# Input columns loaded already turned, row factors applied behind the first projections, in a one-core decoder kernel

## The chip, the cores and the metric

One core of one Trainium2 chip. Times are device microseconds of one execution of the whole program. The median of 3 runs of the kernel before is 974.82 us (974.74 to 976.26). A measurement of this kernel can tell about 0.2% (1.95 us) from no change.

## The reference, cut to what matters

The program runs two decoder blocks, one after the other, over 256 rows of 1024 features (f32). Only the start of the first block bears on this change:

```python
h = jnp.concatenate([filler, meta, x], axis=1)        # 16 meta rows, 256 real rows
u = rms_norm(h, pre_mix_gain)                         # y = x * rsqrt(mean(x*x) + eps) * gain
proj = u @ w_in
qa, ka, va, qb, kb, vb, g = jnp.split(proj, SPLITS, axis=-1)
qa, ka, qb, kb = rope(...)                            # x1*cos - x2*sin, x2*cos + x1*sin
o_swa = windowed_gqa_sink_attention(qa, ka, va, attn_sink, pos, is_real)
o_diff = differential_attention(qb, kb, vb, lam, lambda_init, diff_subln_gain, is_key)
gates = jax.nn.sigmoid(g + b_gate)
merged = g_swa * (o_swa @ w_branch_swa) + g_diff * (o_diff @ w_branch_diff)
```

The norm multiplies each row by one number, the row factor, and each feature by a gain. The row factor can be taken out of the product: (r * x * gain) @ w = r * ((x * gain) @ w).

## The kernel before, in words

**Products.** Every matrix product is made of three products in a reduced float type: weights and activations are each split into a high part (ACT copies the f32 tile into the reduced type, `split` in `scalar`) and a low part (DVE subtracts, `split` in `vector`, line 1338), and TensorE adds high x high, high x low, low x high in PSUM (`feat`, lines 796 to 798; `ropek`, lines 920 to 922 for the first weights). Weights come from DRAM in units of 1 MB, in 4 raw buffers filled by SP's queue (line 2507), and are split in two halves of 128x1024 each into 2 buffers of high and low parts. A half is 24 matmuls of 256 columns (272 where the meta rows take part).

**Order.** `schedule()` writes one list of steps, and each engine walks through it and issues, in that order, what its part of each step is. The engines' queues are in order, so an instruction that waits holds everything behind it on its engine. A "split" step stands where `ahead` puts it: up to four halves ahead of the products, as soon as a buffer is free by the list. Works that lie beside the products are put in by `spread`: a head of attention has the stages s (scores on TensorE), s0/s1 (row maxima on DVE), x0/x1 (exponentials on ACT), n (probabilities on DVE), p0/p1 (transposes, copied out by ACT and by DVE), v (value product), t. The first head of windowed attention starts beside the fourth weights. Steps in `behind_split` come out behind the next splits.

**The head of the kernel.** SP loads X (256 rows), ACT's queue the meta rows, the identity matrix and the gains. ACT and DVE square and sum each row, DVE makes mean + eps, POOL raises it to the power -1/2 (line 2348), ACT and DVE scale the rows. TensorE turns them (line 782), ACT and DVE turn the PSUM banks into the high and low parts of the first activations R1 (lines 1958 and 1328) with the gain. Until then TensorE runs 13 idle matmuls (`keep`, line 787). Unit 0 (queries 0 and 1) is multiplied by `ropek`, unit 1 holds the keys (`rope` "ka0"), unit 2 the values (`v` "va"), unit 3 queries 2 and 3, unit 4 the first gates, unit 5 queries, unit 6 the second gates.

**Rotation.** After a product of queries or keys, ACT copies the four groups of 32 partitions crosswise out of PSUM (`rope` in `scalar`, four instructions), DVE multiplies PSUM by cos and the copy by sin (lines 1421, 1422), POOL adds (line 2360). `swap` makes a copy of the keys with their halves exchanged (ACT, four instructions). Values are copied by ACT, turned by TensorE and copied by DVE (`vt`, lines 1428 to 1434). A gate unit is two halves in one bank, then two tanh on ACT straight from PSUM. `claim` gives PSUM banks: banks 0 to 2 for the products, 3 to 7 for the heads; a claim waits for whatever still reads the bank.

On the profile's pages ACT's instructions all have line 1958 (a helper), so they are told apart by tiles: whi is a split, F<-F a swap, SD<-ps 128x272 a value copy, SE, SC or SD<-ps of 32 partitions a rotation copy.

Of the kernel before, what the change touches and what calls it, by code (L numbers as in the profile page):

```python
# [209 lines left out]
def schedule():  # L210
# [11 lines left out]
    def take(i, j):  # L222
        ahead(taken=1)
        while behind_split:
            step(*behind_split.pop(0))
        halves.append((i, j))
# [140 lines left out]
    def gates(u):  # L367
        return unit(("gate", u), "w_in", "feat", 4608 + 256 * u)
# [15 lines left out]
    va = behind(values("va", 1280, 0), ("swap",), ("setup",))  # L384
    units = [opening(), rope("ka0", 1024, 0), va, qa[1], ga[0], qa[2], ga[1], qa[3], ga[2], qb[0], vb[0], kb[0],
# [6 lines left out]
    n = len(units) * 2  # L392
# [89 lines left out]
def program(nc, A, out):  # L482
    with ExitStack() as ctx:
# [34 lines left out]
        mix_in, band_in = signal("in_mix", 16), signal("in_band", 16)  # L518
# [10 lines left out]
        swap_act, gate_act = signal("swap_act"), signal("gate_act")  # L529
# [70 lines left out]
        xmeta = F[:, 3072:3200].rearrange("p (b n) -> p b n", b=8)  # L600
        xs0 = [F[:, 0:1024], F[:, 1024:2048], F[:, 2048:3072]]
# [47 lines left out]
        def par_of(name):  # L649
# [3 lines left out]
            "n1": (X, xs0, R1, par_of("pre_mix"), "small"), "nm": (memt, xsm, R3b, par_of("g_mem"), "all"),  # L653
            "nx2": (X, xs2, R1, par_of("g_mix"), "all")}
        APART = ("nx2",)
        SOURCE = {"n1": ((x_in, 0), (x1_in, 0), (meta_in, 0)), "nm": ((mem_in, 0), (mem_in, 0)),
# [11 lines left out]

        def row_scale(s):

            return stat((s, "rs"), 2)

        def rows_of(s):
            src, xs = NORM[s][0:2]
            return [(src[:, 0, :], 128), (src[:, 1, :], 128)] + ([(metat, 16)] if s == "n1" else [])
# [92 lines left out]
        def tensor(e, counting):  # L768
# [86 lines left out]
            def turn(s, pairs=(0, 2, 4, 6)):  # L855
                xs, pool = NORM[s][1], NORM[s][4]
                if s == "n1":
                    p.wait_ge(id_in, 0)
# [18 lines left out]
            def turnm():  # L877
                B = claim("small", ("n1", "TX"), (norm_dve, ("n1", "xv")))
                for b in range(8):
                    p.wait_ge(norm_dve, ("n1", "sc", b // 4, 2))  # L880
                    t = tr(B[:, b * 16:(b + 1) * 16], xs0[2][0:16, b * 128:(b + 1) * 128])
                t.then_inc(norm_pe(("n1", "TX")))
# [19 lines left out]
            def rope(key, b, j, i, k):  # L902
                n = ROPE[key][1]
                B = claim("gemm", ("rope", k), (rope_act, k), (rope_dve, ("cos", k)))
                if n > NR:
                    p.wait_ge(norm_dve, ("n1", "lo", 8))
                feat(B[:, 0:n], i, j, R1, n, normed("n1"), ("rope", k))

            def ropek(part, i):

                hi, lo = unit(i)
                p.wait_ge(lo_split, (i, part))
                if part == 0:
                    for k in range(2):
                        claim("gemm", ("rope", k), (rope_act, k), (rope_dve, ("cos", k)))
                for kt in range(4 * part, 4 * part + 4):
                    p.wait_ge(norm_dve, ("n1", "lo", kt))
                    for k in range(2):
                        o, c = ps("rope", k)[:, 0:256], slice(k * 128, k * 128 + 128)
                        e.matmul(o, hi[:, kt, c], R1[0][:, kt, 0:256], start=kt == 0, stop=False)  # L920
                        e.matmul(o, hi[:, kt, c], R1[1][:, kt, 0:256], start=False, stop=False)
                        m = e.matmul(o, lo[:, kt, c], R1[0][:, kt, 0:256], start=False, stop=kt == 7)
                m.then_inc(gemm(("half", i, part), ("unit", i), ("rope", 0), ("rope", 1)))

            def v(key, u, j, i):
                B = claim("gemm", (key, u, j), (val_act, (key, u, j)))
                p.wait_ge(norm_dve, ("n1", "lo", 8))
# [16 lines left out]
            def swa(g, part):  # L944
                kv, x = g // 2, nth["swa", g]
                E = E2[x % 2]
                if part == "s":
                    p.wait_ge(rope_pool, ("qa", g))
                    p.wait_ge(rope_pool, ("ka0", 1))
                    p.wait_ge(swap_act, 1)  # L950
# [78 lines left out]
            def gate(u, j, i):  # L1029
                pair("gate", u, j, i, "gemm", R1, normed("n1"), (gate_act, u))  # L1030
# [284 lines left out]
            parts = {"turn": turn, "turnx": turnx, "rsb": rsb_, "rope": rope, "ropek": ropek, "turnm": turnm, "v": v, "vt": vt, "swa": swa, "diff": diff, "gate": gate, "bsw": bsw, "bdf": bdf,  # L1315
# [3 lines left out]
            keep(banks[7].t, 13, half[:, 0:1].to_broadcast([128, 128]), half[:, 0:1].to_broadcast([128, 256]))  # L1319
# [4 lines left out]
        def vector(e, counting):  # L1324
# [67 lines left out]
            def turnm():  # L1392
                d.wait_ge(norm_pe, ("n1", "TX"))
                d.wait_ge(mix_in, 0)
                e.tensor_tensor(xmeta, ps("n1", "TX")[:, 0:128].rearrange("p (b n) -> p b n", b=8),
                                par("pre_mix", 0, 8).unsqueeze(2).to_broadcast([128, 8, 16]), MUL).then_inc(norm_dve(("n1", "xv")))
                d.wait_ge(norm_act, ("n1", "xhi"))
# [1198 lines left out]
```

## Time and profile before

| what | value |
|---|---|
| median of 3 runs | 974.82 us |
| the profiled execution's own time | 975.47 us |
| its span | 973.7 us |
| granted TensorE clock, mean | 0.998 |
| busy TensorE / DVE / ACT / POOL | 97% / 70% / 54% / 13% |
| DMA, mean over the span | 159 GB/s |
| waits of TensorE, 12.9 to 100 us | one, of 0.76 us, for DVE (ahead of the second weights) |

The span runs from the first to the last instruction; the execution's own time lies 1.8 us above it. Matmuls are pipelined, so the start of one group of matmuls to the start of the next is what is compared here, not busy time. In a timeline row the columns are start, duration, engine, line, operation, out<-in, shapes, count, and in brackets the idle time before it with what ended it.

### The profile page before, as it was taken

How to read it: one execution, taken by the hardware profiler on the slowest of the kernel's cores; microseconds unless marked ns; L12 is line 12 of the kernel's file. 1: busy time of each engine (PE TensorE's matmuls, PEld its weight loads, DVE VectorE, ACT ScalarE, POOL GpSimd, SP SyncE). 2: the span in 40 equal slices, each digit the busy share in tenths (PEclk: the TensorE clock that was granted, in tenths of full speed). 3: DMA queues.
4: the chain of work that ended last, by engine and by line, in shares of the span. 5: the costliest groups of instructions: out<-in, count | busy, mean ns of one | idle time of the engine just before them, and what ended most of it. 6: DMA issues, size and time to landing. Idle time of an engine off the chain costs nothing.

```text
span 973.7 us, 15544 instructions
## 1 busy us (share of the span) xinstructions
PE 948.5 (97%) x6212; PEld 846.2 (87%) x6212; DVE 683.5 (70%) x1251; ACT 527.6 (54%) x1009; POOL 125.4 (13%) x145
## 2 busy tenths in 40 slices
PE   8999999999999999999999999799899999999997
PEld 8999888999999988888888898698699898888885
DVE  5888767777478676666667678786665577676765
ACT  6876666765456643444455786434444354444343
POOL 2211111211032000000001129610100000000001
PEclk9999999999999999999999999999999999999999
DMA  9544434234377556465547652201354445546541
GB/s 317 188 138 131 130 105 156 93 125 132 129 250 242 168 186 216 173 213 169 193 157 242 210 187 88 87 1 44 132 172 130 151 135 210 202 169 204 170 164 43
DMA packets 115864, 154.71 MB, mean 159 GB/s; under 512 B 2729, under 2 KB 98225, under 8 KB 115537
## 3 DMA queue, kind: packets, MB, share of 16 engines
q1 hardware_dynamic: 113376, 142.91, 44.0%
q0 software_dynamic: 1952, 10.42, 3.0%
q8 instruction: 49, 0.80, 0.3%
q10 hardware_dynamic: 464, 0.40, 0.2%
q14 instruction: 23, 0.18, 0.1%
HBM read 150.56 MB, written 3.16 MB: 158 GB/s over the span
## 4 chain that ended last, share of the span: by engine, by line
PE 85%; DVE 8%; ACT 5%; issue 2%; DMA 0%; POOL 0%; POOLq 0%; DVEq 0%; ACTq 0%
PE ps L820 14%; PE ps L796 8%; PE ps L798 8%; PE ps L797 8%; PE ps L821 7%; PE ps L1107 4%; PE ps L1080 4%; PE ps L1081 4%; PE ps L1082 4%; PE ps L839 3%; PE ps L841 3%; PE ps L840 3%; PE ps L782 3%; DVE wlo L1338 2%; PE ps L809 2%; PE ps L811 2%
## 5 line engine op out<-in xcount | busy, mean ns | idle before, releaser
L1338 DVE TENSOR_TENSOR wlo<-raw,whi 128x1024 fp32r<-128x1024 f32 (+1 forms) x268 | 326.8, 1237 | 161.7 <-ACT whi L1958 161.4
L1958 ACT ACTIVATE whi<-raw 128x1024 fp32r<-128x1024 f32 (+1 forms) x268 | 274.2, 1051 | 133.7 <-PE ps L821 53.8
L820 PE MATMUL ps<-R1b,whi 128*128 128x512 f32 x576 | 201.8, 393 | 0.0
L796 PE MATMUL ps<-R1b,whi 128*128 128x256 f32 (+1 forms) x592 | 173.3, 293 | 0.8 <-DVE wlo L1338 0.8
L798 PE MATMUL ps<-R1b,wlo 128*128 128x256 f32 (+1 forms) x592 | 168.3, 284 | 0.0
L797 PE MATMUL ps<-R1b,whi 128*128 128x256 f32 (+1 forms) x592 | 168.2, 284 | 0.0
L821 PE MATMUL ps<-R1b,wlo 128*128 128x256 f32 x576 | 161.4, 280 | 0.0
L820 PEld LDWEIGHTS ps<-R1b,whi 128*128 128x128 f32 x576 | 108.1, 188 | 24.7 <-issue 0.5
L796 PEld LDWEIGHTS ps<-R1b,whi 128*128 128x128 f32 x592 | 112.3, 190 | 10.1 <-issue 7.9
L798 PEld LDWEIGHTS ps<-R1b,wlo 128*128 128x128 f32 x592 | 112.5, 190 | 0.0
L797 PEld LDWEIGHTS ps<-R1b,whi 128*128 128x128 f32 x592 | 112.3, 190 | 0.2
L821 PEld LDWEIGHTS ps<-R1b,wlo 128*128 128x128 f32 x576 | 108.2, 188 | 0.6
L2348 POOL TENSOR_TENSOR st<-st 128x1 f32<-128x1 f32 (+5 forms) x28 | 23.1, 832 | 382.5 <-DVE st L1331 299.8
L1080 PE MATMUL ps<-whi,R3ah 128*128 128x512 f32 x176 | 69.0, 392 | 1.1 <-DVE wlo L1338 1.1
L1081 PE MATMUL ps<-wlo,R3ah 128*128 128x512 f32 x176 | 68.8, 391 | 0.0
L1082 PE MATMUL ps<-whi,R3al 128*128 128x512 f32 x176 | 68.5, 389 | 0.0
L1958 ACT ACTIVATE F<-F 128x512 f32<-128x512 f32 (+6 forms) x58 | 29.3, 507 | 57.2 <-DVE F L1591 53.7
L1958 ACT ACTIVATE R3ah<-F 128x512 fp32r<-128x512 f32 x22 | 13.9, 632 | 67.8 <-DVE F L1613 67.8
L1580 DVE TENSOR_REDUCE F<-ps 128x256 f32<-128x512 f32 x72 | 49.3, 684 | 0.0
L1958 ACT ACTIVATE SC<-ps 128x512 f32<-128x512 f32 (+3 forms) x78 | 33.1, 428 | 22.5 <-PE ps L798 10.4
L1080 PEld LDWEIGHTS ps<-whi,R3ah 128*128 128x128 f32 x176 | 33.0, 188 | 9.1 <-issue 1.9
L1958 ACT ACTIVATE SD<-ps 32x256 f32<-32x256 f32 (+4 forms) x54 | 21.3, 398 | 34.9 <-PE ps L1277 19.3
(293 smaller groups left out, 1800.2 us busy)
## 6 DMA issues: line engine op xcount, KB each, us to landing
raw<-in_w_in SPq DMA_DIRECT2D x34, 1024.0 KB, 5.1
raw<-in_w_ffn_in SPq DMA_DIRECT2D x22, 1024.0 KB, 5.1
raw<-in_w_ffn_out SPq DMA_DIRECT2D x11, 1024.0 KB, 5.3
raw<-in_w_gate SPq DMA_DIRECT2D x11, 1024.0 KB, 5.3
raw<-in_w_up SPq DMA_DIRECT2D x11, 1024.0 KB, 5.3
raw<-in_w_down SPq DMA_DIRECT2D x11, 1024.0 KB, 5.8
raw<-in_w_out SPq DMA_DIRECT2D x8, 1024.0 KB, 5.0
raw<-in_w_xkv SPq DMA_DIRECT2D x8, 1024.0 KB, 5.4
```

The source lines that it names most:

```text
L796: e.matmul(o, hi[:, kt, c], R[0][:, kt, 0:n], start=kt == 0, stop=False)
L797: e.matmul(o, hi[:, kt, c], R[1][:, kt, 0:n], start=False, stop=False)
L798: m = e.matmul(o, lo[:, kt, c], R[0][:, kt, 0:n], start=False, stop=kt == 7)
L820: e.matmul(B[:, :].rearrange("p (a n) -> p a n", a=2), hi[:, kt, c], R[2][:, :, kt, 0:256], start=kt == 0, stop=False)
L821: m = e.matmul(B[:, 0:256], lo[:, kt, c], R[0][:, kt, 0:256], start=False, stop=kt == 7)
L1080: e.matmul(B[:, :], Fh[:, k, c], hi[:, k, d], start=j == 0 and k == 0, stop=False)
L1081: e.matmul(B[:, :], Fh[:, k, c], lo[:, k, d], start=False, stop=False)
L1082: m = e.matmul(B[:, :], Fl[:, k, c], hi[:, k, d], start=False, stop=end and k == 1)
L1107: return e.matmul(o, a, b, start=True, stop=True)
L1338: e.tensor_tensor(half_of(wlo[i % HL], i, k), half_of(raw[i % RAW], i, k), f32(half_of(whi[i % HL], i, k)), SUB).then_inc(lo_split(i, (i, k)))
L1580: e.tensor_reduce(FSLOT[j % 2][0][:, at:at + 256], B[:, :].rearrange("p (a n) -> p n a", a=2), AX, ADD).then_inc(ffn_dve((kind, f, j, b)))
L1958: return e.activation(o, i, f, **kw)
```

## The change

- The host lays out a new input `x_cols`: the gains (8 columns), then X and the meta rows already turned, 128 partitions x 8 blocks x 272 rows. It is loaded in two pieces, the first weights in two halves between them. R1 is made straight from it: ACT makes column x gain in the reduced type, DVE the rest (`xsplit`). The row factor is no longer in R1.
- X, the identity, the cos/sin tables and all parameters are loaded behind the third weights, by SP; the meta rows behind the second, the band table behind the fourth. ACT's queue loads nothing at the start.
- The row factors are made beside the second weights' products (`rowstat`: two squares on ACT, one on DVE, one power on POOL for all rows). Three matmuls spread them along the columns (`rowtab`), DVE multiplies the cos and sin tables by them, and keeps the first 256 for the gates (`rowkeep`).
- Queries and keys get the row factor through the tables, values in the copies behind their transposes (products in place of copies), gates by a new DVE product 128x512 out of PSUM into GA (`scaled`), after which the two tanh run on GA in place.
- `scaled` stands at the beginning of the step behind the gate unit, tanh behind the next splits and what already stands behind them.
- The first four rotation products use the heads' banks. The first rotations (keys' and queries' first blocks) stand before and between the fourth weights' splits, the second ones behind the value product's second half; swap is in two parts. The fifth weights' first split, which stood ahead of the third weights' second half, stands with its second split behind that half and everything that follows it.
- The first weights' products run in the order high x high, high x low, low x high over four blocks, each with its own wait.
- 9 idle matmuls in place of 13.

```diff
     def opening():
+        def laid(k, key, b):
+            step("roped", key, b, k)
+            step("rotate", key, b, k)
         order.append(("w_in", "featk", 0, 256))
         for j in range(2):
             take(0, j)
             step("ropek", j, 0)
-            if j:
-                for b in range(2):
-                    step("roped", "qa", b, b)
-                    step("rotate", "qa", b, b)
-                state["rope"] = 2
             yield 1
+        order.append(("w_in", "feat", 1024, 256))
+        for j in range(2):
+            take(1, j, 4 - j)
+            step("ropep", "ka0", j, j, 1, 3 * j)
+            if j == 0:
+                step("rowstat")
+            else:
+                step("roped", "ka0", 0, 0)
+                step("roped", "qa", 0, 1)
+                step("setup")
+            yield 1
+        state["rope"] = 4
+        order.append(("w_in", "feat", 1280, 256))
+        take(2, 0, 2)
+        step("v", "va", 0, 0, 2)
+        step("rowtab")
+        step("rotate", "ka0", 0, 0)
+        ahead(2)
+        step("rotate", "qa", 0, 1)
+        step("rowkeep")
+        yield 1
+        take(2, 1, 3)
+        step("v", "va", 0, 1, 2)
+        step("swap", 0)
+        laid(2, "qa", 1)
+        laid(3, "ka0", 1)
+        step("swap", 1)
+        step("vt", "va", 0, 0)
+        yield 1
...
     def gates(u):
-        return unit(("gate", u), "w_in", "feat", 4608 + 256 * u)
+        yield from unit(("gate", u), "w_in", "feat", 4608 + 256 * u)
+        step("scaled", u)
+        behind_split.append(("tanh", u))
...
-    step("rows", "n1")
+    step("xsplit", 0, 4)
     ahead(1)
-    step("turn", "n1", (0, 2))
-    ahead(2)
-    step("turn", "n1", (4, 6))
-    step("turnm")
+    step("xsplit", 4, 8)
...
+            def rowtab():
+                B = claim("head", ("row0",), (norm_dve, "kept"))
+                p.wait_ge(id_in, 0)
+                p.wait_ge(norm_pool, "row0")
+                for i in range(2):
+                    mm(B[:, 128 * i:128 * i + 128], rs0[:, i:i + 1].to_broadcast([128, 128]), ident)
+                mm(B[:, 256:NT], rs0[0:16, 2:3].to_broadcast([16, 128]), ident[0:16, 0:16]).then_inc(norm_pe("row0"))
...
-            keep(banks[7].t, 13, half[:, 0:1].to_broadcast([128, 128]), half[:, 0:1].to_broadcast([128, 256]))
+            keep(banks[7].t, 9, half[:, 0:1].to_broadcast([128, 128]), half[:, 0:1].to_broadcast([128, 256]))
...
+            def xsplit(first, end):
+                for kt in range(first, end):
+                    d.wait_ge(norm_act, ("n1", "hi", kt))
+                    stt(R1[1][:, kt, :], xT[:, kt, :], xcols[:, kt:kt + 1], f32(R1[0][:, kt, :]), MUL, SUB).then_inc(
+                        norm_dve(("n1", "lo", kt)))
...
+            def scaled(u):
+                d.wait_ge(gemm, ("gate", u))
+                d.wait_ge(norm_dve, "kept")
+                e.tensor_tensor(GA[:, 2 * u:2 * u + 2, :], ps("gate", u)[:, :].rearrange("p (b n) -> p b n", b=2), rep(rsb0, 2),
+                                MUL).then_inc(gate_dve(u))
...
+            def xsplit(first, end):
+                a.wait_ge(xb_in if first else xa_in, 0)
+                for kt in range(first, end):
+                    act(R1[0][:, kt, :], xT[:, kt, :], scale=xcols[:, kt:kt + 1]).then_inc(norm_act(("n1", "hi", kt)))
...
+            def tanh(u):
+                a.wait_ge(gate_dve, u)
+                a.wait_ge(set_dve, "hb")
+                for k in range(2):
+                    act(GA[:, 2 * u + k, :], GA[:, 2 * u + k, :], ACT.Tanh, bias=hb[:, 2 * u + k:2 * u + k + 1],
+                        scale=0.5).then_inc(gate_act(u))
...
-            e.dma_start(X[:, 0, :], x_src[:, 0, :]).then_inc(x_in(0), 16)
-            e.dma_start(X[:, 1, :], x_src[:, 1, :]).then_inc(x1_in(0), 16)
+            cut = 8 + 4 * NT
+            e.dma_start(xcols[:, 0:cut], A["x_cols"][:, 0:cut]).then_inc(xa_in(0), 16)
             for i in range(len(order)):
                 src, k, n = unit_src(i)
+                dst = raw[i % RAW][:, 0:k * n].rearrange("p (k n) -> p k n", k=k)
+                if i == 0:
+                    e.dma_start(dst[:, 0:4, :], src[:, 0:4, :]).then_inc(first_in(0), 16)
+                    e.dma_start(xcols[:, cut:], A["x_cols"][:, cut:]).then_inc(xb_in(0), 16)
+                    e.dma_start(dst[:, 4:8, :], src[:, 4:8, :]).then_inc(raw_in[0](0), 16)
+                    continue
```

## Rows read from the trace of the kernel before

**Rows 1.** The page's first part: busy time, share of the span, instructions.
```profile
PE 948.5 (97%) x6212; PEld 846.2 (87%) x6212; DVE 683.5 (70%) x1251; ACT 527.6 (54%) x1009; POOL 125.4 (13%) x145
```

**Rows 2.** The chain of waits, 0 to 20 us: start us, us, what.
```profile
0.73 4.26 DMA X<-in_x
...
18.03 1.24 DVE wlo L1338
```

**Rows 3.** Timeline of SP's queue, 0 to 10 us: the first two weight loads' issue.
```profile
1.62 0.43 SPq L2507 DMA_DIRECT2D raw<-in_w_in  x1
...
3.07 0.45 SPq L2507 DMA_DIRECT2D raw<-in_w_in  x1
```

**Rows 4.** DMA view, the same two issues: KB, us from issue to landing.
```profile
raw<-in_w_in SPq DMA_DIRECT2D x1, 1024.0 KB, 8.0
...
raw<-in_w_in SPq DMA_DIRECT2D x1, 1024.0 KB, 10.2
```

**Rows 5.** Timeline of PE, 0 to 79 us: idle matmuls, products, scores, value products.
```profile
0.93 8.52 PE L787 MATMUL ps<-st 128*128 128x256 f32 x26 [0.93 <-DVE st L1946]
...
12.78 0.35 PE L920 MATMUL ps<-R1b,whi 128*128 128x256 f32 x1 [0.85 <-DVE R1b L1328]
...
19.40 0.36 PE L796 MATMUL ps<-R1b,whi 128*128 128x272 f32 x1 [0.76 <-DVE wlo L1338]
...
31.59 0.49 PE L782 MATMUL ps<-ca,SD 128*128 128x128 f32 x3
31.83 0.36 PE L796 MATMUL ps<-R1b,whi 128*128 128x256 f32 x1
...
36.68 0.39 PE L796 MATMUL ps<-R1b,whi 128*128 128x256 f32 x1
...
53.27 0.61 PE L971 MATMUL ps<-SC,SD 128*128 128x128 f32 x4
...
78.22 0.61 PE L971 MATMUL ps<-SC,SD 128*128 128x128 f32 x4
```

**Rows 6.** Timeline of ACT, 26 to 53 us.
```profile
26.95 1.63 ACT L1958 ACTIVATE SE<-ps 32x272 f32<-32x272 f32 x4
...
30.29 1.79 ACT L1958 ACTIVATE F<-F 64x272 f32<-64x272 f32 x4 [0.20 <-POOL F L2360]
...
33.44 1.05 ACT L1958 ACTIVATE whi<-raw 128x1024 fp32r<-128x1024 f32 x1
...
45.78 0.84 ACT L1958 ACTIVATE SE<-ps,st 128x256 f32<-128x256 f32 x2
...
52.34 0.60 ACT L1958 ACTIVATE SC<-ps 128x512 f32<-128x512 f32 x1
```

**Rows 7.** Timeline of DVE, 37 to 79 us.
```profile
37.15 0.42 DVE L1428 COPY F<-ps 128x256 f32<-128x256 f32 x1
...
52.04 0.69 DVE L1468 COPY SC<-ps 128x512 f32<-128x512 f32 x1
52.64 0.28 DVE L1470 COPY SC<-ps 128x128 f32<-128x128 f32 x1
52.84 0.42 DVE L1421 TENSOR_TENSOR SE<-ps,ca 128x256 f32<-128x256 f32 x1
...
77.48 0.28 DVE L1470 COPY SC<-ps 128x128 f32<-128x128 f32 x1
```

**Rows 8.** Timeline of POOL, 29 to 31 us: the sum that swap 1 waits for.
```profile
29.48 0.78 POOL L2360 TENSOR_TENSOR F<-SE 128x272 f32<-128x272 f32 x1 [1.97 <-DVE SE L1422]
```

**Rows 9.** Timeline of PE, 581 to 584 us, and the windows view of one microsecond.
```profile
581.24 1.95 PE L1107 MATMUL ps<-st,F 128*128 128x1 f32 x16
...
583.36 0.41 PE L797 MATMUL ps<-R1b,whi 128*128 128x256 f32 x1
583.58 0.41 PE L798 MATMUL ps<-R1b,wlo 128*128 128x256 f32 x1
...
583.00:584.00 1.00, 1.00 (x6) 1.00 (x6) 0.79 (x3) 0.07 (x1) 0.92 (x1) 0.55 0.07 25
```

More of the change, by code:

```diff
@@ L220, in ahead, with take @@
         step("ahead", len(halves) + n, len(halves) + taken)
-    def take(i, j):
-        ahead(taken=1)
+    def take(i, j, n=2 * HL):
+        ahead(n, 1)
         while behind_split:
@@ L517, in program @@
         x_in, x1_in, meta_in, id_in, pc_in, ca_in = [signal("in_" + n, 16) for n in ("x", "x1", "meta", "id", "pc", "ca")]
-        mix_in, band_in = signal("in_mix", 16), signal("in_band", 16)
+        xa_in, xb_in, first_in, band_in = [signal("in_" + n, 16) for n in ("xa", "xb", "first", "band")]
         cb_in, mem_in, g1_in, g2_in, g3_in = [signal("in_" + n, 16) for n in ("cb", "mem", "g1", "g2", "g3")]
@@ L903, in rope @@
                 n = ROPE[key][1]
-                B = claim("gemm", ("rope", k), (rope_act, k), (rope_dve, ("cos", k)))
-                if n > NR:
-                    p.wait_ge(norm_dve, ("n1", "lo", 8))
+                B = claim("head" if k < 4 else "gemm", ("rope", k), (rope_act, k), (rope_dve, ("cos", k)))
                 feat(B[:, 0:n], i, j, R1, n, normed("n1"), ("rope", k))
@@ L911, in ropek @@
                 hi, lo = unit(i)
-                p.wait_ge(lo_split, (i, part))
                 if part == 0:
                     for k in range(2):
[L915 to L923, printed above, removed]
+                        claim("head", ("rope", 1 + k), (rope_act, 1 + k), (rope_dve, ("cos", 1 + k)))
+                p.wait_ge(hi_split, (i, part))
+                for w, r in ((hi, 0), (hi, 1), (lo, 0)):
+                    if w is lo:
+                        p.wait_ge(lo_split, (i, part))
+                    for kt in range(4 * part, 4 * part + 4):
+                        if r:
+                            p.wait_ge(norm_dve, ("n1", "lo", kt))
+                        elif w is hi:
+                            p.wait_ge(norm_act, ("n1", "hi", kt))
+                        for k in range(2):
+                            m = e.matmul(ps("rope", 1 + k)[:, 0:256], w[:, kt, 128 * k:128 * k + 128], R1[r][:, kt, 0:256],
+                                         start=kt == 0 and r == 0 and w is hi, stop=kt == 7 and w is lo)
+                m.then_inc(gemm(("half", i, part), ("unit", i), ("rope", 1), ("rope", 2)))
             def v(key, u, j, i):
                 B = claim("gemm", (key, u, j), (val_act, (key, u, j)))
-                p.wait_ge(norm_dve, ("n1", "lo", 8))
                 feat(B[:, 0:NT], i, j, R1, NT, normed("n1"), (key, u, j))
@@ L2584 @@
     given = {n: src[n] for n in _BIG}
-    given.update(params=params, const_a=const_a, const_b=const_b)
+    columns = np.concatenate([src[n].reshape(-1, 8, 128).transpose(2, 1, 0) for n in ("x", "meta_tokens")], 2)
+    x_cols = np.concatenate([cols("pre_mix_gain"), columns.reshape(128, 8 * NT)], 1)
+    given.update(params=params, const_a=const_a, const_b=const_b, x_cols=x_cols)
     nc = _bacc.Bacc("TRN2", target_bir_lowering=False, num_devices=1)
```

131 lines of the change are left out of this document (68 added, 63 removed).

## The prediction

> **What bounds the kernel now.** I read the page first: TensorE is busy for 97% of the span [rows 1], so away from the ends a change pays only if it moves TensorE's products forward or takes products away. The products of the matrices stay as they are here; what changes is what stands ahead of them. The chain of waits of the first 20 us [rows 2] shows what the head costs: the chain starts with the input's load, which ends at 4.99, runs through sums, a power, scaled rows and transposes, and reaches the second weights' split at 18.03. The DMA rows [rows 3, 4] give arrivals: first weights issued 1.62, landed 8.0 later, 9.6; second weights 3.07 + 10.2 = 13.3. TensorE's timeline [rows 5] gives the marks to beat: first product 12.78, second weights' products 19.40, third weights done 31.59 (the transposes that begin there follow them), second half of the fourth weights 36.68. ACT, DVE and POOL [rows 6 to 8] matter because TensorE has no reserve against them in the first attention heads: the value product of head 0 starts at 53.27 [rows 5], and the last DVE copy that it needs ends at 52.64 + 0.28 = 52.92 [rows 7]. That is 0.35 us of slack. For head 2 it is 78.22 against 77.48 + 0.28 = 77.76, 0.46 us. So the question is whether DVE and ACT come earlier too, or only TensorE.
>
> **The head, part by part.** The squares, powers, scaled rows, 24 transposes and the meta rows' own turn go away from the path. In their place the first weights wait only for the columns (0.56 MB) and half the weights (0.52 MB). The old first load, 0.52 MB, landed at 4.99; I put the new one at 5.0 and the half weights behind it at 6.5 (the new order without the ACT queue's loads gains some tenths, the longer first piece takes them back). ACT scales four columns, then splits for 1.05 [rows 6]: first product near **7.7** instead of 12.78. The nine idle matmuls left are 18 of the row's 26 passes, 18 x 8.52 / 26 = 5.9, done at 6.8, so they cost nothing.
>
> The second weights are then bound by DMA. Between the two landings 9.6 and 13.3 came 1.05 + 0.28 MB, 0.36 MB/us. Before, 3.56 MB had to land by 13.3; now it is columns 1.12, first weights 1.05, second weights 1.05 = 3.22 MB. 0.34 MB less is 0.95 us: second weights at 12.35. ACT's half split takes 1.05, and from the start of DVE's half to the products is 19.40 - 18.03 = 1.37 [rows 2, 5]. Products of the second weights: 12.35 + 1.05 + 1.37 = **14.8**, a lead of 4.6 us. The first weights' products end near 12.7, so TensorE stands idle for about 2 us ahead of it. Four halves of (31.59 - 19.40) / 4 = 3.05 follow, and the new row-factor matmuls. The trace has none like them; bounds are 0.24 (three transposes, from 31.59 to the next products at 31.83) and 1.0 (six passes at half of the 0.33 that a 256-column pass of the idle matmuls takes), and I take 0.5, as the operands are a transpose's in size. Third weights done at 14.8 + 12.2 + 0.5 = **27.5**, lead 4.1. The squares, the sum and the power that feed the row factors end near 22 (behind the second weights come the third, 1.05 MB, and X, 1.05 MB, so X lands by 18.5; a square is about 1.1, the power under 1) and are hidden under products until 24. The constants, parameters and band table come later on SP's queue, near 20 and 24; the first user of the band is at 39.
>
> **Where ACT gives it back.** This is the decisive step. ACT's queue behind the third weights' products is: value copy, swap 0, rotation copies of the queries' second block, rotation copies of the keys' second block, swap 1, and only then both halves of the fifth weights' split. The value copy is a wait for 27.65, and everything else is queued behind it. From [rows 6]: copy 0.3 (at most a quarter of the rope's 1.63, 0.4), swap half of 1.79 = 0.9, two ropes at 1.6 = 3.2: 32.1. Swap 1 waits for DVE's two products and POOL's sum. Before, the same wait took from 26.95 + 1.63 = 28.58 to 30.29, 1.7 us [rows 6, 8]: 33.8. Swap 1 0.9, two splits 1.0 each: hi halves at 35.7 and 36.75. DVE's second half split then runs to 37.95, and the second value copies [rows 7] start there. Before they started at 37.15. So **DVE is 0.8 us later than before, although TensorE was 4 us earlier**. TensorE itself waits in the first scores, whose banks are freed by these same rotations and value copies, and starts the second half of the fourth weights at about 34.9 (36.68 before): lead 1.8.
>
> From the second value copies on the order on DVE and ACT is the old one: scores' maxima, exponentials, rotation, splits, the probabilities of head 0, all 0.8 later. ACT has no idle time in that stretch that would take up 0.8.
>
> **The gates.** Eight DVE products 128x512 from PSUM are new. Bounds: two 128x256 products of 0.42 each, 0.84, and the 128x512 copy, 0.69, which gives way after 0.60, at 52.64 [rows 7]. I take 0.65. ACT's two tanh (0.84 together [rows 6], 0.75 where the next instruction overlaps them) are as long as before but now stand behind the second head's exponentials. For gate 0 both fall in the worst place: DVE has 0.65 more ahead of head 0's last copies, ACT 0.75 more between those exponentials and the copy at 52.34. Value product of head 0: DVE 52.92 + 0.8 + 0.65 = 54.4; ACT 52.34 + 0.60 + 0.8 + 0.75 = 54.5. Old start 53.27, so **TensorE is 1.2 us late** here, and its whole lead is gone. Gate 1 stands in the same way ahead of head 2: DVE and ACT are by then about 2.0 behind the old times (0.8 + 0.75 + 0.45 for the second tanh), less 0.46 of slack: 1.6. Gates 2 to 7 fall into DVE and ACT idle time (both wait for TensorE for 1 to 2 us per half weights there), I cost them at nothing; without that cover they cost 0.65 each. Value copies that become products by a row factor keep their durations. DVE's two table products, 0.44 each, and the kept row, 0.42, lie in its idle time before 28.
>
> **Sum.** +1.2 at head 0, +0.4 by head 2: +1.6 us on the profiled execution's 975.47 (span 973.7 and 1.8 around it), 977.1. The median of the runs shown is 0.65 below that execution, so 976.4. Errors: arrival of the second weights 0.5 each way, row-factor matmuls 0.2 down to 0.5 up, queue sums on ACT 0.5. A measurement of this kernel can tell about 0.2%, 1.95 us, so this case reaches from no change to just slower.
>
> **Rivals.** (A) *The heads have more slack than I read*, and the lead lives on: TensorE keeps the 1.8 us that it has at the fourth weights (973.0), or, if ACT's queue is not held by the value copy either, up to 4.1 us (970.7). For it speaks that TensorE never waits for long in this stretch before; against it the 0.35 and 0.46 us. It decides where head 0's value product starts: before 53.27. Chance 0.23.
> (B) *The clock falls in the new idle time.* At 581.24 sixteen one-column products took 1.95 us, and then the granted clock was 0.55 of full in the next microsecond [rows 9], the 1.2 GHz level, with products 0.22 apart (583.36 to 583.58). At full clock 24 take 3.05, 0.127 apart. Some 15 products at 0.1 more are 1.5 us. The kernel now has about 2 us of idle TensorE ahead of 14.8, behind a stretch that had small gaps already. If it falls there, the third weights end at 29.0, ACT's queue starts 1.5 later and all behind it: +3.1, 977.9 by the median. Against it: the engine was idle or in transposes from 9.05 to 12.78 before and its products then ran at full clock. Chance 0.27.
> By the Trainium skill (TensorE: Matmul & The Clock Gate, Part 1: The HAM clock gate), TensorE's clock gate passes half the pulses by default and after idling, all of them only once the engine is kept busy. By that rule the time is this rival's 977.9 instead of 976.4, and the four idle matmuls taken away count against the change; the rows from 9.05 to 12.78 disagree, the row at 583 agrees.
> (C) *DVE cannot carry the gates*: all eight products on the path, 8 x 0.65 = 5.2, of which 1.1 is in my sum already: 976.4 + 4.1 = 980.5. Chance 0.05. My own case has the other 0.45. That the head does not start earlier at all cannot be, since the loads on its path are cut.
>
> **Numbers.** Prediction 976.5. Range 972.0 to 979.5: my case, (B) whole, and of (A) the part that keeps no more than about 2.8 us; outside are the rest of (A), about 0.1, and (C) with some tail, about 0.1. Faster by over 0.2% is nearly all of (A): 0.22. Within 0.2%: two thirds of my case and a little of (A) and (B): 0.37. Slower: a third of mine, most of (B), (C): 0.41.
>
> **What would show it.** First product near 7.7, second weights' near 14.8 with 2 us of idle before; third weights done near 27.5; granted clock 1.00 in 14 to 19 (else B); on ACT a wait of over 1 us before swap 1 and the fifth weights' splits only near 34.7; DVE's second value copies near 38; head 0's value product near 54.5, waiting for DVE or ACT; head 2's near 79.8; behind that the old spacing. It is wrong if the fifth weights' splits come before 33, or if head 0's value product starts before 53.3.

## The result, and the profile after

The changed kernel takes 977.88 us (median of 20 runs, 976.70 to 982.11), the kernel before 976.01 beside it (20 runs): ratio 1.0024, 95% interval 1.0015 to 1.0033. On another chip (the last experiment below) it was 1.0030, 1.0019 to 1.0041; one execution there, of 3283.67 us, is in the slow state and left out. So it is slower: both intervals lie clear of 1, and both ratios lie a little above the 0.2% that a measurement can tell, though the lower ends of the intervals do not. A ratio here goes by all executions of a pair, so it is not the quotient of the two medians. The profiled execution is one of the longer ones, 980.79 us with a span of 979.0; the end of this section says where its time went.

The chain of waits of the changed kernel, 12 to 52 us (start us, us, what):

```profile
2.65 10.36 DMA raw<-in_w_in
13.03 1.07 ACT whi L2015
...
15.40 0.40 PE ps L828
...
24.75 0.76 PE ps L1139 x6
...
28.78 0.40 ACT SD L2015
...
33.73 0.44 DVE SE L1470
34.24 0.77 POOL F L2422
35.03 0.43 ACT F L2015
...
35.94 1.07 ACT whi L2015
37.03 0.99 DVE wlo L1370
...
41.12 0.50 DVE SC L1366
```

It reads like the forecast: DMA of the second weights, TensorE until the third are done, then ScalarE's value copy at 28.78, the rotations, GpSimd's sum, swap 1 at 35.03, and only behind that the fifth weights' split, VectorE's half of it, its value copies, and the first maxima at 41.12. The chain of before had the transposes and the input there [rows 2].

TensorE's timeline (start us, us, engine, line, operation; in brackets the idle time before it and what ended it). L828 to L830 are the products' lines, L1139 the row-factor products, L814 transposes, L973 scores, L1003 value products:

```profile
7.88 2.17 PE L954 MATMUL ps<-R1b,whi 128*128 128x256 f32 x16
...
15.40 0.40 PE L828 MATMUL ps<-R1b,whi 128*128 128x272 f32 x1 [1.53 <-DVE wlo L1370]
...
24.59 0.93 PE L1139 MATMUL ps<-ca,st 128*128 128x128 f32 x6
25.44 0.39 PE L828 MATMUL ps<-R1b,whi 128*128 128x272 f32 x1
...
28.58 0.49 PE L814 MATMUL ps<-ca,SD 128*128 128x128 f32 x3
...
33.96 0.69 PE L973 MATMUL ps<-F 64*128 64x272 f32 x2 [0.97 <-DVE SE L1469]
...
35.92 0.72 PE L973 MATMUL ps<-F 64*128 64x272 f32 x2 [1.27 <-DVE SD L1363]
36.58 0.39 PE L828 MATMUL ps<-R1b,whi 128*128 128x256 f32 x1
...
55.98 0.71 PE L1003 MATMUL ps<-SC,SD 128*128 128x128 f32 x4 [0.99 <-DVE SC L1520]
```

Against [rows 5]: first product 12.78, now 7.88; second weights' products 19.40, now 15.40; third weights done 31.59, now 28.58. A lead of 3.0 us. The second half of the fourth weights began at 36.68 and now begins at 36.58: behind the two waits among the scores the lead is 0.1 us. The timelines of ScalarE and VectorE behind it, each in the same columns:

```profile
28.78 0.40 ACT L2015 ACTIVATE SD<-ps 128x272 f32<-128x272 f32 x1 [1.70 <-PE ps L830]
29.20 0.88 ACT L2015 ACTIVATE F<-F 64x272 f32<-64x272 f32 x2
30.11 1.58 ACT L2015 ACTIVATE SD<-ps 32x256 f32<-32x256 f32 x4
31.72 1.63 ACT L2015 ACTIVATE SE<-ps 32x272 f32<-32x272 f32 x4
35.03 0.88 ACT L2015 ACTIVATE F<-F 64x272 f32<-64x272 f32 x2 [1.69 <-POOL F L2422]
35.94 2.01 ACT L2015 ACTIVATE whi<-raw 128x1024 fp32r<-128x1024 f32 x2
```
```profile
37.03 2.36 DVE L1370 TENSOR_TENSOR wlo<-raw,whi 128x1024 fp32r<-128x1024 f32 x2 [1.16 <-ACT whi L2015]
39.30 0.42 DVE L1477 TENSOR_TENSOR F<-ps,st 128x256 f32<-128x256 f32 x1
39.64 1.45 DVE L1363 TENSOR_SCALAR SD<-ps,st 16x128 f32<-16x128 f32 x4
41.12 0.50 DVE L1366 CUSTOM_DVE_ANT_0 SC<-ps,ca,pc 128x272 f32<-128x272 f32 x1
...
52.07 0.69 DVE L1570 TENSOR_TENSOR SE<-ps,pc 128x512 f32<-128x512 f32 x1
...
55.05 0.68 DVE L1518 COPY SC<-ps 128x512 f32<-128x512 f32 x1
55.65 0.28 DVE L1520 COPY SC<-ps 128x128 f32<-128x128 f32 x1
```

The second value copy began at 37.15 [rows 7] and now begins at 39.30; the first maxima began at 38.72 and now at 41.12; the copy of head 0's probabilities began at 52.04 and now at 55.05. Before, the first maxima stood in VectorE's timeline as

```profile
38.72 0.50 DVE L1334 CUSTOM_DVE_ANT_0 SC<-ps,ca,pc 128x272 f32<-128x272 f32 x1
```

TensorE's waits in the changed kernel, 0 to 96 us (total, times, longest):

```profile
PE ps L828 <- DVE wlo L1370: 1.5, 1, 1.5
PE ps L973 <- DVE SD L1363: 1.3, 1, 1.3
PE ps L1003 <- DVE SC L1520: 1.0, 1, 1.0
PE ps L973 <- DVE SE L1469: 1.0, 1, 1.0
...
```

Two waits stand among head 0's scores and one before its value product, which starts at 55.98 (53.27 before, +2.7). Heads 1 and 2 follow at 68.76 and 81.50, 3.0 and 3.3 late. From there to 550 us the distance grows by no more than 0.1. The windows view (the stretch, its length, busy us of PE, PEld, DVE, ACT and POOL; then the granted clock, the DMA share and GB/s) shows one thing that the forecast did not have here, a low clock right behind those scores:

```profile
33.00:37.00 4.00, 1.77 (x7) 1.01 (x8) 2.40 (x7) 2.26 (x5) 1.04 (x2) 1.00 0.67 230
37.00:38.00 1.00, 1.00 (x9) 1.00 (x8) 0.97 (x1) 0.97 (x2) 0.00 (x0) 0.74 0.07 16
38.00:39.00 1.00, 1.00 (x6) 1.00 (x6) 1.00 (x2) 0.95 (x3) 0.00 (x0) 0.50 0.00 0
...
41.00:42.00 1.00, 1.00 (x11) 1.00 (x10) 0.97 (x5) 0.00 (x0) 0.00 (x0) 1.00 1.04 361
```

TensorE was busy for 1.77 of the 4 us from 33 on, and from 37.5 to 40.9 its clock is at the 1.2 GHz level: six products a microsecond in place of eleven. Before, TensorE was busy for all of 33 to 37.

The span is 5.3 us longer than in the profile before (979.0 against 973.7). The 2 us that come behind head 2 lie at 600 to 635, where TensorE waits for VectorE in both kernels, here by 1 us more, and where the clock is 0.57 at 631 to 634. The same kernel was profiled once more (experiment 11) and had no low clock there; where the mean clock of a whole run is 0.993, the kernel before too takes 976.7 to 977.5 and not 974. No verdict below rests on that stretch.

### The profile page after: what moved, and what is told of

Same layout as the page of the kernel before. It is cut to its first block, busy times and chain, and to the rows that moved or that the text cites. A ratio compares the mean times of both kernels' runs of the same rounds, so it can differ in the third digit from the quotient of the medians.

```text
span 979.0 us, 15494 instructions
## 1 busy us (share of the span) xinstructions
PE 950.1 (97%) x6186; PEld 846.9 (87%) x6186; DVE 688.1 (70%) x1255; ACT 527.7 (54%) x1006; POOL 124.4 (13%) x143
## 4 chain that ended last, share of the span: by engine, by line
PE 82%; DVE 9%; ACT 6%; issue 2%; DMA 1%; SPq 0%; POOL 0%; POOLq 0%; DVEq 0%; ACTq 0%
PE ps L852 14%; PE ps L828 7%; PE ps L853 7%; PE ps L830 7%; PE ps L829 7%; PE ps L1139 5%; PE ps L1112 4%; PE ps L1113 4%; PE ps L1114 4%; PE ps L871 3%; PE ps L873 3%; PE ps L872 3%; PE ps L814 3%; DVE wlo L1370 3%; PE ps L841 2%; PE ps L843 2%
## 5 line engine op out<-in xcount | busy, mean ns | idle before, releaser
L828 PE MATMUL ps<-R1b,whi 128*128 128x256 f32 (+1 forms) x592 | 174.1, 294 | 1.5 <-DVE wlo L1370 1.5
L830 PE MATMUL ps<-R1b,wlo 128*128 128x256 f32 (+1 forms) x592 | 169.0, 285 | 0.0
L828 PEld LDWEIGHTS ps<-R1b,whi 128*128 128x128 f32 x592 | 112.9, 191 | 10.9 <-issue 7.4
L830 PEld LDWEIGHTS ps<-R1b,wlo 128*128 128x128 f32 x592 | 113.4, 192 | 0.0
L2406 POOL TENSOR_TENSOR st<-st 128x2 f32<-128x2 f32 (+5 forms) x26 | 21.5, 828 | 397.9 <-DVE st L1363 314.9
```

The lines of the kernel that those rows point to most:

```text
L828: e.matmul(o, hi[:, kt, c], R[0][:, kt, 0:n], start=kt == 0, stop=False)
L830: m = e.matmul(o, lo[:, kt, c], R[0][:, kt, 0:n], start=False, stop=kt == 7)
```

## The experiments

Each ran beside the kernel before: experiments 1, 2, 6 and 7 on one chip, 3 to 5 on a second, 8 and 9 on a third, 10 and 11 on a fourth. Profiles of one stretch can be compared across them only after a look at the second weights' products, which start at 14.54 to 14.93 in the ten experiments with the change in them and at 15.40 in the result's profile.

**1. The fifth weights' split, first half, ahead of swap 1.**
```diff
-        take(2, 1, 3)
+        take(2, 1)
```


> The changed kernel, with the first half of the fifth weights' split put back ahead of the third weights' second half, where ACT waited 1.7 us for TensorE. Theory (the queue of ACT and DVE behind the third weights sets the end): DVE's second value copies start about 1.0 us earlier (39.3 to 38.3), head 0's value product starts near 55.0 instead of 55.98, and the whole is about 1.0 us shorter than the changed kernel. Rival 1 (clock): nothing changes, the scores still wait and the clock still falls near 37; 0.0. Rival 2 (DVE's load of the gates): 0.0, since the work is the same.

Measured: 978.05 against 974.79, ratio 1.0023 (1.0009 to 1.0036), no better than the change. But the step itself did what it should: the maxima start at 39.36 (41.12 in the result's profile, of which 0.8 is the second weights, at 14.61 here; 40.49 in experiment 11; 38.72 before). Head 0's value product starts at 55.34 without any wait, although VectorE's last copy for it ends at 54.37. What holds it is TensorE: the waits of 0.72 and 1.27 among the scores are still there, the clock is low for 6.8 us from 34.7 on, and three halves of products that take 8.7 us at full clock last from 36.50 to 47.45. Here the low clock costs about 0.9 us at head 0.

**2. Idle products in those waits.**
```diff
+                    if x == 0 and u in (1, 2):
+                        keep(B, 2, half[:, 0:1].to_broadcast([128, 128]), half[:, 0:1].to_broadcast([128, 256]))
```


> The changed kernel, with two idle matmuls ahead of the second and of the third score of head 0, where TensorE waits 3.6 us for PSUM banks and the clock then fell to 1.2 GHz for 3.4 us. Rival 1 (the fallen clock costs the time): granted clock stays 1.00 near 37 to 41, and the whole is 1.5 us shorter. Theory: the clock stays up, but head 0's value product still waits for DVE and starts at 55.98 as before; 0.0 within 0.3 us.

Measured: 978.56, ratio 1.0032 (1.0021 to 1.0044). The windows of this kernel, in the same columns:

```profile
33.00:37.00 4.00, 4.00 (x22) 2.86 (x22) 2.75 (x7) 2.79 (x4) 0.76 (x1) 1.00 0.44 148
37.00:38.00 1.00, 1.00 (x11) 1.00 (x10) 1.00 (x2) 0.93 (x4) 0.00 (x0) 1.00 0.00 0
```

The clock stays whole here, and the same halves end at 44.40. (The expectation speaks of 3.6 us of waits; the two are 2.24 together.) It gains nothing, because VectorE is as late as in the changed kernel (maxima 40.26, 1.5 late, plus the gate product: its copy starts at 54.18, 2.1 late). TensorE then waits 0.66, 0.52 and 0.98 for it, and the value product starts at 55.11. So 1.8 of head 0's 2.7 us are VectorE's lateness alone. The other 0.9 is the late load of the result's profile and not its low clock: the second weights' products start 0.86 apart in the two profiles (14.54 and 15.40), the maxima 0.86, the value products 0.87, and both value products wait the same 0.98 to 0.99 us for VectorE.

**3. Both together.** The two diffs above in one kernel.

> The changed kernel with two edits at once: the first half of the fifth weights' split ahead of the second swap, and idle products in TensorE's two waits among head 0's scores. Theory: the loss is VectorE's lateness at head 0, 1.5 us at the maxima (40.26 against 38.72) plus 0.6 of the gate product; with the split early the maxima came at 39.36 (0.6 late) but TensorE had lost 3.4 us to a low clock, which hid it; without the idle products the second edit alone left the maxima at 40.26. Together: no low clock before 60 us, maxima near 39.1 to 39.4, head 0's value product 53.9 to 54.3 (55.98 in the changed kernel, 53.27 before), and a time 1.2 to 1.7 us under the changed kernel's. Rival, that the gate product alone sets head 0: value product still at 55 or later.

Measured: 978.38 against 975.02, ratio 1.0023 (1.0009 to 1.0037): a miss. The clock stays whole up to 627 us, but the maxima start at 40.02 and not at 39.4, and the value product at 54.88. ScalarE's rows, here and in experiment 1, show where the 0.66 us come from:

```profile
27.89 1.06 ACT L2017 ACTIVATE whi<-raw 128x1024 fp32r<-128x1024 f32 x1 [1.39 <-DMA raw<-in_w_in]
```
```profile
27.22 1.06 ACT L2015 ACTIVATE whi<-raw 128x1024 fp32r<-128x1024 f32 x1 [0.95 <-DMA raw<-in_w_in]
```

The early split stands ready for weights that have not landed. They were issued at 16.72 here and at 15.75 in experiment 1, behind the load of a table, and everything behind that split on ScalarE and VectorE is 0.66 to 0.67 late. So this profile's miss says nothing against the sum of the two edits; it shows that at this early place the split hangs on when its weights land.

**4. The order itself.** Query 1's copies move behind the set-up, its rotation into the first value half, swap 1 two half units on:
```diff
                 step("setup")
+                step("roped", "qa", 1, 2)
...
         step("rowkeep")
+        step("rotate", "qa", 1, 2)
...
         step("swap", 0)
-        laid(2, "qa", 1)
-        laid(3, "ka0", 1)
-        step("swap", 1)
         step("vt", "va", 0, 0)
+        laid(3, "ka0", 1)
...
-    at += [(n - 6, 1, ("between",))]
+    at += [(n - 6, 1, ("between",)), (7, -1, ("swap", 1))]
```


> The changed kernel with its own part undone otherwise: query 1's rope copy right behind the set-up and its rotation ahead of the second value unit, the second swap two units later, so that the fifth weights' split does not queue behind it. Theory: ScalarE begins that split near 31.8 (35.9 in the changed kernel), VectorE's second value copies end near 37, the maxima start at or before 38.7 if TensorE's scores are there (its scores no longer wait: the 0.97 and 1.27 waits are gone and the clock stays whole), head 0's value product 53.0 to 53.9, and the time 1.8 to 3 us under the changed kernel's, so within 1 of the kernel before, on either side. Rival, that order does not matter since other waits take over: no more than 0.5 better.

Measured: 975.64 against 975.02, ratio 0.9999 (0.9985 to 1.0013), the kernel before's time. ScalarE's, VectorE's and TensorE's timelines in this kernel:

```profile
29.53 1.63 ACT L2015 ACTIVATE SE<-ps 32x272 f32<-32x272 f32 x4
31.19 2.00 ACT L2015 ACTIVATE whi<-raw 128x1024 fp32r<-128x1024 f32 x2
...
35.19 0.89 ACT L2015 ACTIVATE F<-F 64x272 f32<-64x272 f32 x2 [0.40 <-POOL F L2422]
```
```profile
33.31 2.93 DVE L1370 TENSOR_TENSOR wlo<-raw,whi 128x1024 fp32r<-128x1024 f32 x2
...
37.98 0.50 DVE L1366 CUSTOM_DVE_ANT_0 SC<-ps,ca,pc 128x272 f32<-128x272 f32 x1
...
51.90 0.68 DVE L1518 COPY SC<-ps 128x512 f32<-128x512 f32 x1
```
```profile
32.62 1.26 PE L973 MATMUL ps<-F 64*128 64x272 f32 x4 [0.31 <-DVE SD L1363]
...
52.83 0.71 PE L1003 MATMUL ps<-SC,SD 128*128 128x128 f32 x4 [0.99 <-DVE SC L1520]
```

The split starts at 31.19 in place of 35.94, swap 1 now waits 0.40 with nothing urgent behind it, the maxima start at 37.98, the scores' waits are gone but for 0.3, and the clock is whole from 0 to 966 us. Head 0's value product starts at 52.83, 0.4 ahead of the old place, 3.2 ahead of the result's profile and 2.6 ahead of experiment 11, whose second weights' products start at 14.78 as they do here (14.82). It still waits 0.99 for VectorE, which is now busy from 33.31 to 44.2 without a gap. Of the 4.75 us by which the split comes earlier, 0.6 is the second weights; 1.6 is query 1's four copies and 2.6 swap 1 with its wait, which both stood ahead of the split. Reordering these steps, with no work taken away, takes the whole loss back, and that shows the cause. The edit moves both at once, so it does not say what either would give alone. This kernel ends the first half of the fourth weights' products 3.6 us ahead of the kernel before (31.17 against 34.73), and of that the heads leave nothing: VectorE sets them.

**5. The gate products by themselves,** added to the kernel before:
```diff
+                e.tensor_tensor(GA[:, 2 * u:2 * u + 2, :], ps("gate", u)[:, :].rearrange("p (b n) -> p b n", b=2),
+                                ones[:, 0:1].unsqueeze(2).to_broadcast([128, 2, 256]), MUL).then_inc(gate_dve(u))
```


> The kernel before with one part of the change: VectorE multiplies each gate's products from PSUM by ones into SBUF (same shape as the change's product) and ScalarE's tanh reads that one half unit later. Theory (forecast): 0.6 us a head that carries a gate in its stretch where VectorE is what TensorE waits for; head 0's value product has VectorE's copy right behind (52.92 against TensorE's 53.27), so 0.3 to 0.6 there, 53.5 to 53.9; whole time +0.3 to +1.0. Rival, that the gates are most of the loss: +2 or more. Rival, that they are covered: within 0.2.

Measured: 976.94 against 975.02, ratio 1.0010 (0.9997 to 1.0024). Value products of heads 0, 1 and 2 start at 53.47, 66.23 and 78.97 in place of 53.27, 65.75 and 78.22: 0.20, 0.48 and 0.75 late, and not later behind that. (Its second weights' products start 0.1 early, so the price is nearer to 0.3, 0.6 and 0.8.)

**6. Gates without the row factor.** VectorE's eight products are left out and tanh reads PSUM, so the gates lack the rows' factor.

> The changed kernel without the row factor on the gates: the eight DVE products 128x512 are left out and tanh reads PSUM. Theory: only gates 0 and 1 lie on the path, so 0.7 to 1.3 us shorter than the changed kernel. Rival 2 (DVE carries the gates badly all along): up to 5 us shorter. Rival 1 (clock): 0.0.

Measured: 979.29 against 974.79, ratio 1.0035 (1.0021 to 1.0048), a miss as a time. Its profile has head 0's value product at 54.84, with 0.5 of that from earlier weights (second weights' products at 14.87) and 0.6 from the gate. TensorE's two waits among the scores and the low clock behind them are unchanged. Later it gives back what it gained: tanh, which now reads PSUM itself, still stands behind the next splits, and behind the last gate TensorE waits for it, where the changed kernel has no wait.

```profile
263.97 0.38 PE L840 MATMUL ps<-R3bh,whi 128*128 128x256 f32 x1 [0.46 <-ACT SE L2014]
```

Against the profile before it is 2.6 us late behind head 2 and 3.2 behind this wait (the changed kernel 2.8 at both in experiment 11). The clock then falls for 3.4 us at 586.6 and for 6.8 us at 627.5. The gates are thus not the bulk of the loss.

**7. All gate products one half unit later.**

> The changed kernel, with every gate's DVE product and its tanh one half unit later, so that they stand behind head 0's last copies. Theory: head 0's value product starts 0.7 us earlier (55.98 to 55.3), heads 1 and 2 with it, 0.7 to 1.2 us shorter in all. Rival 1 (clock): 0.0. Rival 2 (DVE's load as such): 0.0, since DVE does as much as before, only later.

Measured: 984.00, ratio 1.0085 (1.0071 to 1.0099): 5 to 6 us worse than without. Head 0's value product gained (54.68), but the last gate's product is wanted at once by the merge, and moved it comes 2.1 us late there. TensorE:

```profile
265.83 0.43 PE L845 MATMUL ps<-R3bh,whi 128*128 128x256 f32 x1 [2.06 <-DVE SE L1574]
```

A low clock of 3.4 us follows that wait; together they take the distance to the kernel before from 3.0 to 6.6 us. This profile shows one thing more. TensorE's two waits among head 0's scores are there as in the changed kernel (0.97 and 1.26), and the clock does not fall behind them:

```profile
33.00:37.00 4.00, 2.46 (x13) 1.71 (x14) 2.75 (x8) 2.61 (x4) 0.76 (x1) 1.00 0.48 163
37.00:38.00 1.00, 1.00 (x11) 1.00 (x11) 1.00 (x2) 0.95 (x3) 0.00 (x0) 1.00 0.00 0
```

Even so its value product waits 0.39 us for VectorE.

**8, 9. More room on VectorE.** On top of the reordered version, the second value unit's transposes and copies two half units later, behind the first maxima; then gate 0's product alone behind head 0's copies as well.
```diff
-    qa[1] = behind(qa[1], ("vt", "va", 0, 1))
...
+           (8, 1, ("vt", "va", 0, 1))
...
+           (11, -1, ("scaled", 0)), (11, 0, ("tanh", 0))
```


> The reordered version with one more move: the second value unit's transposes and VectorE's copies of it (0.41 + 1.45 us) two half units later, behind the first maxima of head 0. Theory, that VectorE's queue sets head 0 (it is busy without a gap from 25 to 44 us, then idle 0.83, then busy to the copy at 51.90 that TensorE waits 0.99 for): the maxima start 1.9 earlier at 36.1, the copies fill the 0.83 idle, the copy of the probabilities comes 0.8 earlier (51.1), head 0's value product 52.0, and the time 0.5 to 0.9 under the reordered version's. Rival, that TensorE sets it: its value product stays at 52.8 and the time within 0.3.

> As the one before, and gate 0's product alone moved behind head 0's copies of the probabilities (all other gates where the change has them). Theory, that the 0.69 us gate product costs what it takes ahead of those copies and nothing elsewhere: copies 0.6 earlier (50.5), head 0's value product 51.3 to 51.6, time 0.4 to 0.7 under the one before and 1 to 2 us under the kernel before. Rival, that the gate product's place costs nothing here and head 1 or gate 1 gives back what head 0 gains (as where all gates were moved, +2.1 us at the last): the same time as the one before or longer.

Measured: 975.71 and 974.86 against 975.86; ratios 0.9992 (0.9982 to 1.0002) and 0.9997 (0.9985 to 1.0009). Head 0's value product starts at 52.28 and 51.62 (53.27 before): the first moved by 0.55 where 0.8 was expected, the second by 0.66 as expected. But heads 1 and 2 then stand 0.7 and 0.4 ahead of the kernel before in both, and 0.3 of that lasts. As a time the second is a miss (1 to 2 us under the kernel before were expected; its ratio is not clear of 1). In it TensorE waits 0.40 for VectorE again at head 1, as its rival has it: VectorE's work only changes places.

**10. Gates 0 to 2 off VectorE:** ScalarE copies them out of PSUM, GpSimd multiplies, tanh comes later.

> The version with the second value copies later, and the products of gates 0 to 2 taken off VectorE: ScalarE copies them from PSUM, GpSimd multiplies by the row factors (its rotations of 128x256 take 0.74 alone and up to 1.69 us beside VectorE, so some 1.5 to 3.4 for 128x512), tanh comes two half units later. Theory, that VectorE's time in heads 0 to 2 gives back what head 0 gains: value products of heads 0, 1 and 2 at about 51.7, 64.3 and 76.8 (52.28, 65.04 and 77.79 where VectorE has them), time 0.5 to 1 under that version's and 1 to 2 under the kernel before. Rival, that GpSimd's long operation slows VectorE's operations beside it by as much as it takes off: the same time within 0.3.

Measured: 976.90 against 976.18, ratio 1.0006 (0.9996 to 1.0016). No faster, so the theory is out. The rival holds in the trace: no head gains, with value products at 52.66, 65.25 and 77.82 against 52.28, 65.04 and 77.79 in experiment 8. VectorE's and GpSimd's timelines:

```profile
50.58 1.03 DVE L1366 TENSOR_SCALAR st<-st 128x2 f32<-128x2 f32 x1
```
```profile
50.30 1.29 POOL L2444 TENSOR_TENSOR SE<-SE,pc 128x512 f32<-128x512 f32 x1 [2.58 <-ACT SE L2018]
```

An operation on two numbers a row, 0.17 us elsewhere, takes 1.03: it ends when GpSimd's product of 1.29 does. Value product 52.66, 0.4 worse than with the gate on VectorE.

**11. The change once more,** beside the kernel before on the last chip.

> The changed kernel as it is, once more, beside the kernel before on this chip, since the comparison of the result was on another. Theory: the same profile up to 60 us (TensorE's waits of 0.97 and 1.27 among head 0's scores, the clock at half for 3.4 us soon behind them, head 0's value product near 56), ratio 1.002 to 1.004. Rival, that the low clock ahead of 60 us was of that one execution: whole clock there, head 0's value product near 55.

Measured: 979.02 against 976.18, ratio 1.0030 (1.0019 to 1.0041). The waits of 0.97 and 1.26 among the scores are the same. The clock is low again, for 6.8 us from 34.9 on, inside the second wait, and head 0's value product starts at 55.42, 0.11 behind the end of VectorE's last copy for it (0.05 in the result's profile). Five profiles have these two waits (the result's and experiments 1, 6, 7 and 11), and four of them show the fall. So it comes often and not always. This execution has no other fall before 966 us.

## Why the prediction was right, and where it was not

The time, 976.5 with a range of 972.0 to 979.5, holds 977.88. The largest chance (0.41) was on slower by over 0.2%; the own case, +1.6 us, lay just under that line, and the measured ratio, 2.3 us, is just over it. The mechanism was right and one term was too small.

*What bounds the kernel* held: TensorE's busy share is 97% again, and the loss is where the 0.35 us of slack was read.

*The head* came out within a few tenths: first product 7.88 (7.7). Second weights' products 15.40 (14.8): the load took 10.36 us from its issue and landed at 13.0, not 12.35. In the ten experiments on the changed kernel they start at 14.54 to 14.93, so the step was right and this one execution late. The row-factor products took 0.85 (24.59 to 25.44) for the 0.5 assumed, near the upper bound. Third weights done 28.58 (27.5), lead 3.0 (4.1). The lead at the fourth weights was put at 1.8 us and was 0.1 (36.58): beside those 1.1 us the waits among the scores were longer than taken.

*ScalarE's queue*, called the decisive step, was right in each link: value copy, swap, ropes, a wait of 1.69 for GpSimd's sum (1.7), swap 1, splits. They came at 35.94, not 34.7, and nearly all of the difference is the 1.1 us of the head. Experiment 4, which changes only this order, shows that it is the cause: 975.64.

*The mis-sized term* is VectorE's lateness ahead of head 0: forecast 0.8 from the second value copies on, measured 2.15 there (39.30 against 37.15) and 2.40 at the maxima (41.12 against 38.72). 0.86 of it is only this profile's late load: experiment 2, with the second weights in time, has 1.5 at the maxima. Followed there link by link, the value copy on ScalarE starts 0.26 later than forecast (27.91 for 27.65; in it are the row-factor products' 0.35 and second weights that are 0.3 early), the split 0.36 (35.06 for 34.7), the second value copies 0.48 (38.43 for 37.95) and the maxima 0.74. The last step is a sentence that was wrong: "value copies that become products by a row factor keep their durations". Four of them on 16 rows take 1.45 us, the copies took 1.21. The forecast also says that ScalarE has no idle time in that stretch. It has, 2.29 and 2.02 us before the change, but waiting for VectorE's statistics, so VectorE's lateness passes through whole. It is 2.40 at the maxima and, with the gate product's 0.6, 3.01 at the copy (55.05 against 52.04). Less the 0.35 of slack that is 2.66, and head 0 is 2.7 late.

*The gates*: 0.69 us, giving way after 0.60, as taken (0.65). Its effect was overstated at head 0 and right in sum: experiment 5 has 0.2 to 0.3 there and 0.8 by head 2, since before the change TensorE had the 0.35 of slack. "Gates 2 to 7 cost nothing" was right from gate 3 on.

*Sum*: head 0 late by 2.7 (1.2 forecast), head 2 by 3.3 (1.6) in the profile; 2.2 and 2.7 in experiment 11, where the load was in time. 2.3 is a fair figure for whole runs. At a mean clock of 0.996 to 0.997 the changed kernel took 976.7 to 977.7 and the kernel before, at 0.997, 974.3 to 975.1 but for one execution of 976.1.

*Rival A*, the lead lives on, is out for the change: the value product starts at 55.98. Experiments 8 and 9 show how little of it can live: of a lead of 3.6 us at the fourth weights 0.3 to 0.4 is left behind head 2.

*Rival B*, the clock falls in new idle time, was right as a mechanism and wrong in its place and price. The idle time that it named, ahead of the second weights (1.1 to 1.5 us), brought no fall; the clock was 1.00 there in every run. It fell at the scores of head 0, where TensorE was busy for 1.77 us of four, and the prediction knew of these waits and priced them at nothing for the clock. Experiments 2 and 4, which take the idle time away in different ways, have no fall there, and neither has experiment 7, which keeps it. The price was put at 3.1 us. At head 0 of the changed kernel it is 0.1 us at most, since VectorE is later still: the result's profile and experiment 2, with and without the fall, differ there by 0.87 where their second weights differ by 0.86, and experiment 11's value product starts 0.11 behind VectorE's copy. In experiment 1, where VectorE is earlier, it costs 0.9. The Trainium skill (TensorE: Matmul & The Clock Gate, Part 1: The HAM clock gate) has the gate set by how busy TensorE has been; by that rule the trace agrees at 37.5, and experiment 7 shows that the same waits need not bring a fall. Of the rival's evidence against itself one reading is off: the transposes begin at 9.29 and not at 9.05, with one idle piece of 0.85 us ahead of 12.78.

*Rival C* is out: the eight gate products cost about 0.8, not 5.2.

What stays open: how much of experiment 6's time its wait at 263.97 and its low clocks explain, why the clock does not always fall at head 0's scores, and what decides whether it falls between 580 and 640 us, where it did in both kernels' first profiles and in seven of the eleven experiments' and did not in four.

## What to carry to other kernels

A lead on the engine that bounds the kernel is worth only what the helpers' queues let through. Before moving work to the front, walk each helper's queue in program order from the first new wait to the next thing that the bounding engine needs; here a swap, with the wait for its input, and one query's copies stood in front of a split that everybody needed, and moving them gave back the whole loss of 2.3 us. When a helper has no gap left, moving its work from one place to another moves the wait to the next stage.

## What the runs showed of the hardware that was not expected

Products by a per-row factor are not free in place of copies: four on 16 partitions by 128 took 1.45 us for 1.21, while the product 128x512 from PSUM took 0.69, as the copy did.

GpSimd blocks VectorE's smallest operations: 0.17 us became 1.03 beside a product of 1.29 in experiment 10. It goes both ways: in experiment 4 two splits took 2.93 us (2.36 in the changed kernel at 37.03) and the rotation beside them 1.69 (0.76 in the changed kernel at 34.24). The Trainium skill (SBUF — State Buffer, SBUF: two separate sides) describes the port pair of the two as a lock held for a whole instruction, not a share of bandwidth; by that rule the trace agrees, since the small operation ends at 51.61 and GpSimd's at 51.59.

The clock fell at two idle pieces of 0.7 to 1.3 us among short scores in four profiles of five, and behind one of 2.06 us in experiment 7, and in no profile behind the 1.1 to 1.5 us that stand between two long rows of products. What a fall costs depends on who is later at the next meeting: at head 0 3.4 to 6.8 us at half clock cost 0.1 us at most where VectorE was later, and 0.9 where it was not.
